# Banded attention in a two-layer trunk: mask matmuls ahead of the scores, next pair's scores ahead of this pair's values, two value banks

## The chip, the cores and the metric

One core of a Trainium2 chip runs the whole program. The metric is device time in microseconds (us), the median of several executions. The engines are TensorE (PE, with its weight loads as PEld), VectorE (DVE), ScalarE (ACT), GpSimd (POOL) and SyncE (SP), which issues the weight DMAs.

## What is computed

Two layers of a decoder trunk, 512 tokens by 1024 channels in f32. Each layer mixes tokens by three branches side by side, then runs an MLP:

```python
o_a = mla_branch(...) @ w_o_mla          # 8 heads, causal
o_b = swa_branch(q_swa, k_swa, v_swa, positions, swa_sinks) @ w_o_swa   # the banded branch
o_c = stick_breaking_branch(...) @ w_o_sb
x = x + rms_norm((g0 * o_a + g1 * o_b + g2 * o_c) @ w_out)
x = x + rms_norm(square(relu(rms_norm(x) @ w_up)) @ w_down)
```

The banded branch has 8 query heads of 64 channels, a window of 128 tokens, and one learned sink for each head:

```python
s = einsum(q, k) * HEAD_DIM ** -0.5          # a block of 128 queries sees itself and the block before
s = where(valid, s, -inf)
m = maximum(max(s), sink)
p = exp(s - m); p = p / (sum(p) + exp(sink - m))
o = einsum(p, v)
```

## The kernel before

Every engine's instruction list is written out by hand, and engines meet through counting semaphores. Nothing reorders the work: an engine that waits holds all that is queued behind it. Every f32 matmul is three matmuls of high and low parts (`three`), so most operands need a high part, written by ACT, and a low part, written by DVE. Weights stream through a ring of four chunks. `split` on ACT writes the high part of a chunk (128x1024), `split` on DVE the low part.

The **banded stage** lies between the eight causal heads and the stick-breaking stage. Its heads are called m = 0 to 7 here, in four pairs t = 0 to 3. The program's `n` in this stage is 2t. Beside the heads, PE runs two output tiles of the causal branch (`out_tile(0, ..)`) and one projection tile of 24 matmuls for each pair. The work on one head goes round the engines like this:

- PE, `band_scores(t)`: scores of both heads of a pair. Their matmuls use 64 rows of the array each, and the heads alternate between the two halves. Masks are added by matmuls of 128 rows with an identity.
- DVE, `band_biggest(m)`: four instructions for the maximum over the score banks (`bmx`). POOL then reduces it over partitions (`bmxr`), and PE subtracts it from the scores (`band_shift(m)`).
- ACT, `soft_exp` (`bs_f`) and `band_hi` (`bp_hi`). DVE, `band_lo` (`bp_lo`). There is one `bp_hi` and one `bp_lo`: `band_hi(m)` waits until `band_values(m-1)` on PE has read them.
- PE, `band_values(m)`: values into half a bank, and the sum of the probabilities into the other half.
- DVE, `band_den(m)`: adds `sink_exp(m)` of ACT to that sum. ACT, `soft_out(m)`: logarithm and exponential of it (`dn`). DVE, `soft_out(m)`: their product with the values (`of`), which frees the value bank. After each odd head `out_hi` on ACT and `out_lo` on DVE split `of`.
- `mixed` on DVE multiplies an output tile by its gate and frees the tile's bank.

POOL's maximum for head m also waits for `sink_exp(m-2)`. Eight PSUM banks exist. Banks 2 to 5 hold the scores of a pair, bank 6 (`pv_bank`) the values, and bank 7 the results of `rotate`, which turns query channels for the rotary part (`rope`, `rope_in`, `rope_turn`, `rope_out` on ACT and DVE). In the stick-breaking stage bank 7 holds scores again. That stage starts on DVE with `stick_min(0)` and `stick_min(1)`, and its first values matmul (`stick_values(0)`, L885) waits for the low part of its probabilities (`p_lo`), which is at the end of a chain over DVE and ACT.

## Time and profile before

| | |
|---|---|
| median of 3 runs | 1734.01 us (1733.11 to 1734.31) |
| the profiled execution's own time | 1734.41 us |
| its span, first to last instruction | 1732.6 us |
| PE busy | 98% of the span |
| DVE, ACT, POOL busy | 64%, 49%, 8% |
| mean granted TensorE clock | 0.997 of full speed |
| banded stage, first layer | about 162 to 240 us of the span |
| banded stage, second layer | about 1018 to 1096 us of the span |

Busy shares are averages over the whole span. Matmuls overlap each other's ends in the records, so the distance between the starts of two matmuls is what one costs in a stream. The same holds for DVE and ACT: the start-to-start distance is the cost in a queue, and the duration counts when another engine waits.

### The profile page before, as it was taken

What the parts mean: (1) busy time and instruction counts of PE and PEld (TensorE: products, weight loads), DVE (VectorE), ACT (ScalarE), POOL (GpSimd) and SP (SyncE); (2) the same over time, 40 slices, a digit from 0 to 9 for tenths busy, and PEclk for the clock granted to TensorE, in tenths of its full rate; (3) what the DMA queues carried; (4) which work ended last, traced back from release to release, by engine and by line L of the source; (5) the groups of instructions that cost most, each with busy time, mean ns of one, the idle gap of its engine ahead of it and who ended that gap; (6) DMA issues with size and microseconds to landing.
All of it is one profiled execution on the core that took longest, in us unless ns stands there. A gap on an engine that the chain in (4) does not pass through costs nothing.

```text
span 1732.6 us, 21793 instructions
## 1 busy us (share of the span) xinstructions
PE 1704.3 (98%) x8585; PEld 1437.6 (83%) x8585; DVE 1107.1 (64%) x1498; ACT 854.7 (49%) x1203; POOL 142.0 (8%) x140
## 2 busy tenths in 40 slices
PE   9999999999999999999999999999999999999997
PEld 6888888888898888888888888888888988888886
DVE  8887887775566534364587777877754665344545
ACT  7576666665355414131466755666644554232223
POOL 0111211111100000000001111111111000000000
PEclk9999999999999999999999999999999999999999
DMA  4121121222432222222321211122224122222222
GB/s 149 67 73 59 60 74 62 77 75 80 138 118 74 97 98 97 98 98 97 119 82 65 76 61 61 61 74 74 74 85 164 68 98 97 98 97 98 97 98 73
DMA packets 47495, 152.09 MB, mean 88 GB/s; under 512 B 5153, under 2 KB 9633, under 8 KB 47394
## 3 DMA queue, kind: packets, MB, share of 16 engines
q1 hardware_dynamic: 45664, 147.42, 24.5%
q10 hardware_dynamic: 1730, 3.28, 0.5%
q8 instruction: 68, 1.11, 0.3%
q14 instruction: 33, 0.27, 0.1%
HBM read 146.49 MB, written 4.19 MB: 87 GB/s over the span
## 4 chain that ended last, share of the span: by engine, by line
PE 83%; issue 7%; DVE 6%; ACT 3%; POOL 1%; DMA 1%; DVEq 0%; SPq 0%; ACTq 0%; POOLq 0%
PE bank L579 77%; PE bank L584 3%; PE bank L834 1%; PE bank L885 1%; POOL mix L2303 1%; ACT w_hi L1039 1%; DVE w_lo L1582 0%; DVE h_lo L1617 0%; DVE hf L1629 0%; PE bank L588 0%; DMA x<-in_x 0%; PE bank L687 0%; DVE x L1638 0%; DVE fb L1828 0%; ACT dn L1096 0%
## 5 line engine op out<-in xcount | busy, mean ns | idle before, releaser
L579 PE MATMUL bank<-h_hi,w_hi 128*128 128x512 f32 (+1 forms) x1224 | 477.7, 390 | 4.6 <-DVE h_lo L1617 2.4
L579 PE MATMUL bank<-h_hi,w_lo 128*128 128x512 f32 (+1 forms) x1224 | 472.3, 386 | 0.0
L579 PE MATMUL bank<-h_lo,w_hi 128*128 128x512 f32 (+1 forms) x1224 | 472.3, 386 | 0.0
L1039 ACT ACTIVATE w_hi<-raw 128x1024 fp32r<-128x1024 f32 (+2 forms) x269 | 271.0, 1013 | 220.0 <-DMA raw<-in_w 219.6
L1582 DVE TENSOR_TENSOR w_lo<-raw,w_hi 128x1024 fp32r<-128x1024 f32 (+2 forms) x269 | 316.8, 1181 | 63.3 <-ACT w_hi L1039 56.9
L579 PEld LDWEIGHTS bank<-h_hi,w_hi 128*128 128x128 f32 x1224 | 230.4, 188 | 54.8 <-issue 5.7
L579 PEld LDWEIGHTS bank<-h_hi,w_lo 128*128 128x128 f32 x1224 | 230.3, 188 | 46.9
L579 PEld LDWEIGHTS bank<-h_lo,w_hi 128*128 128x128 f32 x1224 | 230.5, 188 | 45.2 <-issue 1.7
L579 PE MATMUL bank<-u_hi,w_hi 128*128 128x512 f32 (+1 forms) x560 | 208.0, 371 | 0.0
L579 PE MATMUL bank<-u_hi,w_lo 128*128 128x512 f32 (+1 forms) x560 | 207.7, 371 | 0.0
L579 PE MATMUL bank<-u_lo,w_hi 128*128 128x512 f32 (+1 forms) x560 | 207.7, 371 | 0.0
L579 PEld LDWEIGHTS bank<-u_lo,w_hi 128*128 128x128 f32 x560 | 105.5, 188 | 18.3
L579 PEld LDWEIGHTS bank<-u_hi,w_hi 128*128 128x128 f32 x560 | 105.5, 188 | 18.1
L579 PEld LDWEIGHTS bank<-u_hi,w_lo 128*128 128x128 f32 x560 | 105.5, 188 | 18.0
L1903 DVE TENSOR_TENSOR usq<-relu 128x512 f32<-128x512 f32 x64 | 44.3, 692 | 104.0 <-ACT relu L1243 103.4
L1243 ACT ACTIVATE relu<-bank 128x512 f32<-128x512 f32 x48 | 28.6, 596 | 139.0 <-PE bank L579 139.0
L1921 DVE TENSOR_TENSOR y<-bank,y 128x512 f32<-128x512 f32 x32 | 22.1, 692 | 98.7 <-PE bank L579 98.7
L579 PE MATMUL bank<-o_hi,w_hi 128*128 128x512 f32 x192 | 76.5, 398 | 0.0
L1245 ACT ACTIVATE u_hi<-relu 128x512 fp32r<-128x512 f32 x64 | 40.5, 633 | 70.1 <-DVE relu L1898 68.6
L579 PE MATMUL bank<-o_hi,w_lo 128*128 128x512 f32 x192 | 74.9, 390 | 0.0
L579 PE MATMUL bank<-o_lo,w_hi 128*128 128x512 f32 x192 | 74.8, 390 | 0.0
L2303 POOL TENSOR_TENSOR mix<-mix,gate 128x512 f32<-128x512 f32 x32 | 44.4, 1391 | 357.0 <-DVE gate L1878 357.0
(264 smaller groups left out, 2747.3 us busy)
## 6 DMA issues: line engine op xcount, KB each, us to landing
raw<-in_w SPq DMA_DIRECT2D x251, 512.0 KB, 3.2
x<-in_x SPq DMA_DIRECT2D x16, 256.0 KB, 3.3
side_raw<-in_w SPq DMA_DIRECT2D x6, 512.0 KB, 4.8
x_spill<-x ACTq DMA_DIRECT2D x8, 256.0 KB, 2.5
x<-x_spill SPq DMA_DIRECT2D x8, 256.0 KB, 3.2
out_y<-x SPq DMA_DIRECT2D x8, 256.0 KB, 2.1
raw<-in_w SPq DMA_DIRECT2D x8, 192.0 KB, 2.4
raw<-in_w SPq DMA_DIRECT2D x8, 128.0 KB, 2.3
```

Source lines behind the costliest of these rows:

```text
L579: mm = pe.matmul(o, s, m, start=start and i == 0 and j == 0, stop=last and i == n - 1 and j == 2, skip_group_check=True)
L584: return pe.matmul(o, stationary, moving, start=False, stop=True, skip_group_check=True)
L834: return pe.matmul(to[:, off + col:off + col + w], a, m, start=(r, n, i) in STICK_STARTS, stop=i == 2, skip_group_check=True)
L885: mm = pe.matmul(pv_bank[:, q0:q0 + w], v[:, j, h % 2, :], part[:, s], start=i == 0 and part is p_hi, stop=part is p_lo, skip_group_check= ...
L1039: act.activation(chunk_in(gc, w_hi, side_hi)[:, 0:w], chunk_in(gc, raw, side_raw)[:, 0:w], ACT.Copy)\
L1243: act.activation(relu[:, n % 2, :], tile_bank(name)[:, :], ACT.Relu).then_inc(free_of(name), 1)
L1245: act.activation(u_hi[g % 2][:, t, :], relu[:, n % 2, :], ACT.Square).then_inc(u_h.sem, 1)
L1582: dve.tensor_tensor(chunk_in(gc, w_lo, side_lo)[:, 0:w], chunk_in(gc, raw, side_raw)[:, 0:w], chunk_in(gc, w_hi, side_hi)[:, 0:w].bitcast( ...
L1903: dve.tensor_tensor(usq[:, n % 2, :], relu[:, n % 2, :], relu[:, n % 2, :], ALU.mult)\
L1921: ins = dve.tensor_tensor(y[:, t, :], tile_bank(name)[:, :], y[:, t, :], ALU.add)
L2303: pool.tensor_tensor(mix[:, t, :], mix[:, t, :], gated_at(b, t), ALU.add).then_inc(mix_add.sem, 1)
```

## The change

The diff touches four things. The masks of a pair are written first, with `start=True`, and the score matmuls add to them. `band_scores(t+1)` stands ahead of `band_values(n)` and `band_values(n-1)` behind `out_tile(0, n)`. Heads 0, 2 and 4 put their values in bank 7, the others in bank 6. ACT and DVE get another order, in which the normalisation of a head stands later and the splits of the weights behind both exponentials. `rotate(2)` moves into the middle of a projection tile.

```diff
+        def values_bank(n):
+            return bank[7] if n - HEADS in (0, 2, 4) else pv_bank
+        def values_bank_free(n):
+            m = n - HEADS
+            if m in (0, 2):
+                return rot_used(m // 2 + 4)
+            return pv_free(n - 1 if 0 < m < 6 else n)
...
                 def band_scores(t):
+                    pe.wait_ge(*p_exp(banks_of(HEADS + 2 * t)))
+                    for r in range(2):
+                        add(band[r][0][:, :].rearrange("p (a c) -> p a c", a=2), cst[:, IDENT, :],
+                            both.unsqueeze(1).broadcast_to([P, 2, 2 * P]), start=True)
+                        add(band[r][1][:, 0:2 * P], cst[:, IDENT, :], both, start=True)
+                        add(band[r][1][:, 2 * P:3 * P], cst[:, IDENT, :], cst[:, MASK_CAUSAL, :])
                     pe.wait_ge(*rpo_l(t + 2))
-                    pe.wait_ge(*p_exp(banks_of(HEADS + 2 * t)))
...
 # stick_scores(0)
+                        pe.wait_ge(*pv_free(HEADS + 5))
...
 # PE, the stage
-                    rotate(2)
-                    tile(("swa_q", 2), h_hi, h_lo)
+                    tile(("swa_q", 2), h_hi, h_lo, None, lambda: rotate(2))
                     for t in range(PAIRS):
                         n = 2 * t
+                        out_tile(0, n)
                         if t:
                             band_values(n - 1)
-                        out_tile(0, n)
                         band_shift(n)
                         out_tile(0, n + 1)
                         band_shift(n + 1)
...
+                            band_scores(t + 1)
                         band_values(n)
-                        if t + 1 < PAIRS:
-                            band_scores(t + 1)
...
 # ACT, the stage
-                            soft_out(HEADS + n - 1)
+                            band_hi(n - 1)
+                            soft_out(HEADS + n - 2)
+                            sink_exp(n - 1)
                         soft_exp(HEADS + n)
                         band_hi(n)
+                        if t:
+                            soft_out(HEADS + n - 1)
+                        sink_exp(n)
+                        soft_exp(HEADS + n + 1)
                         if t:
                             out_hi(HEADS + n - 1)
                         split(C["o", 0, t] + 2)
...
-                        soft_exp(HEADS + n + 1)
-                        sink_exp(n)
...
+                    band_hi(HEADS - 1)
+                    soft_out(2 * HEADS - 2)
+                    sink_exp(HEADS - 1)
...
 # DVE, the stage: see its rows below; behind its loop
+                    band_lo(HEADS - 1)
+                    band_den(HEADS - 2)
+                    soft_out(2 * HEADS - 2)
```

PE's list around the scores of pair 1, before: the scores with their masks in two places (`cst` is the identity), then the values of head 1.

```order
L806 MATMUL bank<-wq_hi,wk_hi 128x256 [waits p_exp,rope_out_lo]
...
L806 MATMUL bank<-wq_hi,wk_lo 128x256 x2
L584 MATMUL bank<-cst 128x512 x2
L806 MATMUL bank<-wq_hi,wk_hi 128x256 x2
...
L806 MATMUL bank<-wq_hi,wk_lo 128x128 x2
L584 MATMUL bank<-cst 128x256
L584 MATMUL bank<-cst 128x128
L584 MATMUL bank<-cst 128x256
L584 MATMUL bank<-cst 128x128
L579 MATMUL bank<-bp_hi,wv_hi 128x256 [waits pv_free,p_lo_ready]
```

The same place in the changed kernel.

```order
L595 MATMUL bank<-cst 128x512 [waits p_exp]
L595 MATMUL bank<-cst 128x256
L595 MATMUL bank<-cst 128x128
L595 MATMUL bank<-cst 128x512
L595 MATMUL bank<-cst 128x256
L595 MATMUL bank<-cst 128x128
L825 MATMUL bank<-wq_hi,wk_hi 128x256 [waits rope_out_lo]
...
L825 MATMUL bank<-wq_hi,wk_lo 128x256 x2
...
L825 MATMUL bank<-wq_hi,wk_lo 128x128 x2
L590 MATMUL bank<-bp_hi,wv_hi 128x256 [waits rot_used,p_lo_ready]
```

The six mask matmuls stand in front of the first wait for the rotated queries. The scores then run without a break, and the values that follow are those of head 0, which wait for bank 7 instead of bank 6.

DVE's list for pair 1 before, from the maximum of head 2 to the end of the two splits (`dn<-bank,dn` is `band_den`, `of` is `soft_out`, `mix` is `mixed`, `w_lo` the splits).

```order
L1692 TENSOR_TENSOR bmx_125<-bank,bmx_125 128x128 [waits max_step,score_full]
L1782 TENSOR_TENSOR dn<-bank,dn 64x512 [waits sink_exp,pv_full]
L1688 TENSOR_SCALAR bmx_126<-bank,vec_all 128x256 [waits score_full,max_all]
...
L1692 TENSOR_TENSOR bmx_126<-bank,bmx_126 128x128 [waits max_step,score_full]
L1791 TENSOR_TENSOR mix<-bank,mix 128x512 [waits mix_gate,tile_full]
L1701 TENSOR_TENSOR of<-bank,dn 64x512 [waits o_lo_ready,den_inv]
L1669 TENSOR_TENSOR bp_lo<-bs_f_121,bp_hi 128x896 [waits p_hi_ready]
L1708 TENSOR_TENSOR o_lo_82<-of,o_hi_81 128x512 [waits o_hi_ready]
L1582 TENSOR_TENSOR w_lo<-raw,w_hi 128x1024 [waits w_hi_ready] x2
L1791 TENSOR_TENSOR mix<-bank,mix 128x512 [waits mix_gate,tile_full]
L1767 TENSOR_TENSOR rb<-bank,cf 128x512 [waits rope_sum,rotated]
```

The same pair in the changed kernel.

```order
L1706 TENSOR_TENSOR bmx_125<-bank,bmx_125 128x128 [waits max_step,score_full]
L1683 TENSOR_TENSOR bp_lo<-bs_f_122,bp_hi 128x896 [waits p_hi_ready]
L1796 TENSOR_TENSOR dn<-bank,dn 64x512 [waits sink_exp,pv_full]
...
L1706 TENSOR_TENSOR bmx_126<-bank,bmx_126 128x128 [waits max_step,score_full]
L1715 TENSOR_TENSOR of<-bank,dn 64x512 [waits o_lo_ready,den_inv]
L1805 TENSOR_TENSOR mix<-bank,mix 128x512 [waits mix_gate,tile_full]
L1796 TENSOR_TENSOR dn<-bank,dn 64x512 [waits sink_exp,pv_full]
L1683 TENSOR_TENSOR bp_lo<-bs_f_121,bp_hi 128x896 [waits p_hi_ready]
L1715 TENSOR_TENSOR of<-bank,dn 64x512 [waits o_lo_ready,den_inv]
L1722 TENSOR_TENSOR o_lo_82<-of,o_hi_81 128x512 [waits o_hi_ready]
L1805 TENSOR_TENSOR mix<-bank,mix 128x512 [waits mix_gate,tile_full]
L1596 TENSOR_TENSOR w_lo<-raw,w_hi 128x1024 [waits w_hi_ready] x2
```

The low part of head 1 (`bp_lo<-bs_f_122`) now lies between the two maxima. `out_lo` (`o_lo_82`) and `mixed` of the second tile stand in front of the splits, and both products `of` stand behind the second maximum.

ACT's list for the same pair before (`bs_f` is `soft_exp`, the two rows on `dn<-dn` are `soft_out`, `dn<-bmxr` is `sink_exp`, `o_hi` is `out_hi`, `w_hi` the splits).

```order
L1094 ACTIVATE dn<-dn 64x512 [waits pv_free,denominator]
L1096 ACTIVATE dn<-dn 64x512 [waits den_inv]
L1123 ACTIVATE bs_f_121<-bank 128x512 [waits score_shifted,p_lo_ready]
...
L1130 ACTIVATE bp_hi<-bs_f_121 128x896 [waits pv_full,p_exp]
L1112 ACTIVATE o_hi_81<-of 128x512 [waits pv_free]
L1039 ACTIVATE w_hi<-raw 128x1024 [waits loaded2]
L1039 ACTIVATE w_hi<-raw 128x1024 [waits loaded3]
L1123 ACTIVATE bs_f_122<-bank 128x512 [waits score_shifted,p_lo_ready]
...
L1105 ACTIVATE dn<-bmxr_127,vec_all 64x512 [waits den_inv,max_all]
```

The same pair in the changed kernel.

```order
L1140 ACTIVATE bp_hi<-bs_f_122 128x896 [waits pv_full,p_exp]
L1104 ACTIVATE dn<-dn 64x512 [waits pv_free,denominator]
...
L1115 ACTIVATE dn<-bmxr_128,vec_all 64x512 [waits den_inv,max_all]
L1133 ACTIVATE bs_f_121<-bank 128x512 [waits score_shifted,p_lo_ready]
...
L1140 ACTIVATE bp_hi<-bs_f_121 128x896 [waits pv_full,p_exp]
L1104 ACTIVATE dn<-dn 64x512 [waits pv_free,denominator]
L1106 ACTIVATE dn<-dn 64x512 [waits den_inv]
L1115 ACTIVATE dn<-bmxr_127,vec_all 64x512 [waits den_inv,max_all]
L1133 ACTIVATE bs_f_122<-bank 128x512 [waits score_shifted,p_lo_ready]
...
L1122 ACTIVATE o_hi_81<-of 128x512 [waits pv_free]
L1049 ACTIVATE w_hi<-raw 128x1024 [waits loaded2]
L1049 ACTIVATE w_hi<-raw 128x1024 [waits loaded3]
```

`soft_out`, `sink_exp` and the second `soft_exp` now stand in front of `out_hi`, and the splits behind all of them.

## Rows read from the trace of the kernel before

**Rows 1.** Waits of PE, whole span: total us, times, longest.

```profile
PE bank L885 <- issue: 2.7, 2, 1.3
...
PE bank L579 <- DVE of L1701: 1.9, 6, 0.5
...
PE bank L834 <- ACT bs_f L1123: 1.2, 2, 0.6
```

**Rows 2.** Timeline of PE, pair 1: start us, duration, instruction, idle before.

```profile
184.12 0.28 PE L579 MATMUL bank<-bp_hi,wv_hi 128*128 128x256 f32 x1
...
185.37 0.27 PE L579 MATMUL bank<-bp_hi,wv_lo 128*128 128x128 f32 x1
185.58 0.38 PE L806 MATMUL bank<-wq_hi,wk_hi 64*128 64x256 f32 x2
185.80 0.28 PE L806 MATMUL bank<-wq_lo,wk_hi 64*128 64x256 f32 x2
...
186.48 0.73 PE L584 MATMUL bank<-cst 128*128 128x512 f32 x2
187.14 0.39 PE L806 MATMUL bank<-wq_hi,wk_hi 64*128 64x256 f32 x2
...
187.97 0.68 PE L584 MATMUL bank<-cst 128*128 128x256 f32 x4
189.16 0.36 PE L579 MATMUL bank<-bp_hi,wv_hi 128*128 128x256 f32 x1 [0.51 <-DVE of L1701]
```

**Rows 3.** Timelines of POOL and PE at the shift of head 1.

```profile
175.79 1.78 POOL L2292 PARTITION_ALL_REDUCE bmxr<-bmx  x1 [5.88 <-DVE bmx L1692]
...
177.63 0.69 PE L584 MATMUL bank<-bmxr,cst 128*128 128x256 f32 x4
```

**Rows 4.** Timeline of DVE, one of each kind of instruction.

```profile
188.94 1.06 DVE L1688 TENSOR_SCALAR bmx<-bank,vec_all 128x256 fp32r<-128x256 f32 x2
...
190.95 0.69 DVE L1782 TENSOR_TENSOR dn<-bank,dn 64x512 f32<-64x512 f32 x1
...
197.50 2.35 DVE L1582 TENSOR_TENSOR w_lo<-raw,w_hi 128x1024 fp32r<-128x1024 f32 x2
...
200.37 0.68 DVE L1767 TENSOR_TENSOR rb<-bank,cf 128x512 f32<-128x512 f32 x1
...
203.26 0.69 DVE L1663 SCALAR_TENSOR_TENSOR tmp<-bank,rstd_x 128x512 f32<-128x512 f32 x1
...
236.91 0.68 DVE L1791 TENSOR_TENSOR mix<-bank,mix 128x512 f32<-128x512 f32 x1
237.63 0.70 DVE L1782 TENSOR_TENSOR dn<-bank,dn 64x512 f32<-64x512 f32 x1
238.36 1.09 DVE L1669 TENSOR_TENSOR bp_lo<-bs_f,bp_hi 128x896 fp32r<-128x896 f32 x1
```

**Rows 5.** Timeline of ACT, one of each kind of instruction.

```profile
193.89 0.98 ACT L1123 ACTIVATE bs_f<-bank 128x512 f32<-128x512 f32 x2 [0.91 <-PE bank L584]
194.90 0.95 ACT L1130 ACTIVATE bp_hi<-bs_f 128x896 fp32r<-128x896 f32 x1
195.76 0.61 ACT L1112 ACTIVATE o_hi<-of 128x512 fp32r<-128x512 f32 x1
...
205.66 0.63 ACT L1094 ACTIVATE dn<-dn 64x512 f32<-64x512 f32 x1
...
206.98 0.72 ACT L1105 ACTIVATE dn<-bmxr,vec_all 64x512 f32<-64x512 f32 x1
```

**Rows 6.** Timelines of DVE, then PE, from the first `stick_min` to `stick_values(0)`.

```profile
240.30 3.13 DVE L1819 TENSOR_SCALAR fb<-bank 128x512 f32<-128x512 f32 x6
...
251.24 0.69 DVE L1663 SCALAR_TENSOR_TENSOR tmp<-bank,rstd_x 128x512 f32<-128x512 f32 x1 [0.50 <-PE bank L579]
...
266.92 1.49 DVE L1669 TENSOR_TENSOR p_lo<-fb,p_hi 128x1280 fp32r<-128x1280 f32 x1 [0.33 <-ACT p_hi L1201]
...
268.51 0.47 PE L885 MATMUL bank<-p_hi,sb_v 128*128 128x512 f32 x1 [1.34 <-issue]
```

More of the change, by code:

```diff
@@ L742, in values @@
                             probs = p_hi[:, s], p_lo[:, s]
-                        mm = three(pv_bank[:, q0:q0 + w], [(vals(j), probs)], start=i == 0)
+                        mm = three(values_bank(n)[:, q0:q0 + w], [(vals(j), probs)], start=i == 0)
                     mm.then_inc(pv_full.sem, 1)
@@ L1700, in soft_out @@
                     own = rows if n < HEADS else slice(0, HEAD)
-                    dve.tensor_tensor(of[rows, :], pv_bank[own, :], dn[own, :], ALU.mult)\
+                    dve.tensor_tensor(of[rows, :], values_bank(n)[own, :], dn[own, :], ALU.mult)\
                        .then_inc(pv_free.sem, 1)
@@ L2112, in _ @@
                         if t:
-                            band_den(n - 1)
+                            band_lo(n - 1)
+                            band_den(n - 2)
+                        band_biggest(n + 1)
+                        if t:
+                            soft_out(HEADS + n - 2)
                         else:
@@ L2133, in _ @@
                             stick_scaled(0, t - 1)
-                        band_den(n)
-                        band_lo(n + 1)
-                        soft_out(HEADS + n)
-                        if 0 < t < 3:
                             stick_in_low(0, t - 1)
+                    band_lo(HEADS - 1)
+                    band_den(HEADS - 2)
+                    soft_out(2 * HEADS - 2)
                     for p in range(PAIRS):
```

34 lines of the change are left out of this document (13 added, 21 removed).

## The prediction

> **What bounds the kernel now.** PE is busy for 98% of the span, so a change in this stage is worth what it takes from PE's stream, or from whatever PE waits for at the end of it. I read the waits of PE over the whole span first. The reader is to see how little there is, and where [rows 1]: 1.9 us before `band_values`, put down to the product that frees the one value bank, 1.2 us at the start of the stick-breaking scores, and 2.7 us at `stick_values(0)`. Each occurs in both layers, and the timelines of both layers agree within some tenths of a us, so I work on the first layer and double the result.
>
> Second, PE's own timeline through pair 1 [rows 2]. It shows small gaps that count as busy. From the last values matmul (185.37) to the first score matmul (185.58) it is 0.21 us, and to the next weights (185.80) 0.22, where a 256-column matmul costs 0.12 and a 128-column one 0.11. So passing between 128-row and 64-row matmuls costs about 0.1 for the switch and 0.1 for the restart, 0.2 in all. It happens four times for each pair: scores, masks (186.48), scores (187.14), masks (187.97).
>
> Third, the end. `stick_values(0)` starts at 268.51 after 1.34 us without a matmul [rows 6]. The `p_lo` it needs starts at 266.92 and takes 1.49. DVE's chain to that point starts with `stick_min(0)` at 240.30, and its last wait for PE is at 251.24 (0.50 us, for a projection tile). From there on DVE and ACT only wait for each other. So what PE gains in the banded stage reaches the end only if DVE's `stick_min(0)` also comes earlier, and if it comes more than 0.5 us later, the rest is lost on the path. This wait decides the change, and it ends last at DVE.
>
> **PE's part of the change.** Masks first leaves two of four switches: 4 pairs x 2 x 0.2 = 1.6 us in a layer. The waits before `band_values` go (about 1 us in a layer), and the wait before the stick-breaking scores may (0.6) [rows 1]. The masks also cover a short wait before pair 0's scores, and `rotate(2)` inside a tile covers another, together about 0.8 by the gaps of PE there, the least certain term. PE's side is thus worth up to 4 us in a layer. No matmul is added or removed.
>
> The Trainium skill, TensorEngine Tiling (Array Packing), under Key Properties, says that a change of tiling mode drains TensorE. The rows agree, with the 0.2 us above, and it would favour this change; it says nothing of who waits next.
>
> **Where pair 0 returns its gain.** The shift of head 1 waits for POOL: its reduction runs 175.79 to 177.57 and the shift starts at 177.63 [rows 3]. DVE reaches that maximum by instructions which the change leaves in order, none of which waits for PE. So PE arrives earlier and waits, and the tile ends where it ended, 184.12 [rows 2]. All of pair 0's lead is gone.
>
> **Walk through pair 1.** Costs: maximum 2.01 (188.94 to 190.95), two splits 2.27, one rotary turn with the copy to ACT and `mixed` 2.89 (200.37 to 203.26), `mixed` 0.6 if the next may overlap it [rows 4]. ACT: two exponentials 1.01, `band_hi` 0.95, `soft_out` 1.32, sink 0.75, `out_hi` 0.52 before the next and 0.61 to its end [rows 5]. Handing over between engines costs 0.04 to 0.1.
>
> From 184.12: masks 0.86 (the 1024 and 768 columns of [rows 2] without the restarts), switch 0.1, scores 1.44: they end at 186.51 (before: 188.5). Values of head 0 run to 188.18. Head 1: `band_hi` 188.28 to 189.23, `band_lo` 189.27. DVE has finished the maximum of head 2 by then, so this start is set by PE and ACT. From here the new order binds:
>
> - `band_lo(1)` then `band_den(0)`. Does the second overlap the first? [rows 4] show `mixed` (0.68) then `band_den` at +0.72 and `band_den` (0.70) then `band_lo` at +0.73: no overlap around an instruction on the upper 64 rows. So 1.09 + 0.04 = 1.13, and `band_den(0)` ends at 190.40 + 0.69 = 191.09. With overlap (0.6 kept as for other pairs, a saving of 0.08 to 0.12) it would be 190.97. I take the first.
> - ACT then does, without a gap, `soft_out(0)`, sink, exponential, `band_hi`, `soft_out(1)`, sink, exponential: 1.32 + 0.75 + 1.01 + 0.98 + 1.32 + 0.75 + 0.98 = 7.11, plus 0.04. `out_hi(1)` starts at 198.24, and DVE, which has nothing to do from about 197.2, gets `out_lo(1)` at 198.89. That is a wait of 1.6 us that DVE did not have.
> - `out_lo` 0.6, `mixed` 0.6, splits from 200.1 to 202.37, rotary turn without `mixed` 2.89 to 205.26, `tmp` and the copy on ACT 1.40, low part 0.6: the maximum of head 4 starts at 207.27.
>
> In the kernel before, that maximum starts only after the same instructions and PE's scores, about a us later. But PE now has the scores of pair 2 at 204.2, and DVE is 3 us behind it. Pair 2's `band_lo(3)` comes at 207.27 + 2.01 = 209.28 and ends at 210.4, while PE, with values and an output tile, stands at `band_values(3)` from 208.5: a new wait of about 1.9.
>
> The Trainium skill, VectorE: DVE Perf Modes, in the section on two Vector instructions with no wait between them, says that an instruction starts only after all earlier ones when its start quadrant differs from theirs. The rows around `band_den` agree with it. By the rule the three `band_lo`, `band_den` pairs give 5.0 us in all for the two layers; with overlap they give 4.4.
>
> **The added waits.** `rotate(4)` now waits for the product of head 0 (193.6, PE comes at 195.8), and behind it stand a tile and scores. Head 2's values wait for the first step of the rotary turn (203.1, PE comes at 204.3). `stick_scores(0)` waits for the product of head 4 (230.4, PE at about 235). All three are hidden by 1.2 us or more. SP's list is not touched; a weight chunk is fetched when PE has done with the one four before, so its fetch moves with PE. The splits stand up to 2.5 us later on DVE, and are done 2 to 3 us before PE asks for them.
>
> **Pairs 2 and 3.** The same chain from maximum to maximum: 2.01 + 1.13 + 0.69 (end of `band_den`) + 7.15 + 0.65 (`out_lo`) + 1.2 + 2.27 + 1.4 + 0.6 = 17.1. Maximum of head 6 at 224.4. PE, with its waits behind it, stands ready again for pair 3. Pair 3 has no `tmp`: its splits end at 224.4 + 15.1 = 239.5. Now `band_lo(7)`, `band_den(6)` and `soft_out(6)` stand behind the splits, where before they stood among PE's last tiles: 1.13 + 0.69 + 0.04 + 1.31 (ACT) + 0.04 + 0.61 = 3.8. `stick_min(0)` starts at 243.3, against 240.30: 3.0 late. PE also waits before `band_values(6)`, since heads 5, 6 and 7 share bank 6 and `soft_out(5)` ends near 234.5; it still starts the stick-breaking scores some 0.5 earlier than before, and that lead is worth nothing.
>
> **Sum.** 3.0 late at `stick_min(0)`, less 0.5 that DVE waited for PE at 251.24 [rows 6], is 2.5 at `p_lo` and at `stick_values(0)`. Behind it PE's stream has no gap of that size in this layer, so it stays. Two layers: +5.0 on the profiled execution's 1734.4, 1739.4; the median before is 0.4 lower, so 1739.0. The bounds of each handover (0.04 or 0.1, overlap or not, ten of them in a layer) move it by 0.8 a layer: +3.4 to +6.6. Errors in my durations lean to neither side, and I give 1738.8.
>
> **Rivals.**
> - **PE's gains stand (faster).** If DVE and ACT keep up, that is if the chain above takes 15 us and not 17.1 from maximum to maximum, `stick_min(0)` comes with PE. PE gains up to 4 in a layer, of which pair 0's 1 or so is lost at POOL: -3 in a layer, 1728; with a part of it 1731. For it: DVE is busy 64% over the span only, and 1.6 us of my chain is one wait. Against: DVE's own instructions for pair 1 sum to 16.6 us (maxima 4.0, low parts 2.2, `band_den` 1.4, products 1.3, `mixed` 1.3, `out_lo` 0.6, splits 2.3, turn 2.2, inputs of the next stage 1.3) of a period near 18. It decides where `out_lo` waits less than 0.3 us. Chance 0.15.
> - **A wash.** DVE is late by 0.5 to 2.2 at `stick_min(0)`, which the waits at 251.24 and a shorter chain nearly take up: 1734 to 1737.4. It needs each pair 0.4 shorter than I have it. Chance 0.24.
> - **Worse.** The late DVE also delays `stick_tail` on PE and the weight splits behind it, so that a chunk is missing later: +8 or more, 1742. Chance 0.06.
> - My forecast, +3.5 to +7: 0.55.
>
> **Range and chances.** Bounds of the forecast 1737.4 to 1740.6; to leave out 2 in 10 I go to 1730 for most of the faster case and 1741.5. A measurement of this kernel tells 0.2%, 3.5 us, from no change. Slower by more than that 0.61, within it 0.25, faster 0.14.
>
> **What would show it.** Right: DVE waits over 1 us before `o_lo` in pairs 1 to 3 (it has no such wait before); PE waits at `band_values(3)` and `band_values(6)`; `stick_min(0)` near 243 and `stick_values(0)` near 271; six masks in a row before each pair's scores. Wrong: `stick_min(0)` before 241, or no wait before `o_lo`. What would make it wrong most easily is ACT: if its seven instructions overlap more than [rows 5] show, each pair gives back up to 1 us.

## The result, and the profile after

The changed kernel takes 1742.5 us (median of 4 executions, 1742.3 to 1743.4); the kernel before took 1733.6 in the same turns. The ratio is 1.0052, with a 95% interval of 1.0037 to 1.0066: 8.9 us slower. The forecast was 1738.8 with a range of 1730 to 1741.5, so the sign was right and the size was outside the range.

All times of a trace count from its own start, and the trace of after shows the first rows of the banded stage 0.62 us earlier than that of before, for reasons ahead of the stage. I add 0.62 where I compare the two.

The head of the page after:

```profile
span 1740.5 us, 21785 instructions
PE 1700.2 (98%) x8585; PEld 1437.1 (83%) x8585; DVE 1107.6 (64%) x1498; ACT 855.0 (49%) x1203; POOL 143.6 (8%) x140
```

The shares of busy time are those of before. What moved is which waits there are. The waits of PE over the whole span, as in [rows 1] (total, times, longest):

```profile
PE bank L590 <- DVE ra L1774: 4.8, 2, 2.6
...
PE bank L590 <- DVE bp_lo L1683: 3.3, 4, 1.5
PE bank L590 <- DVE of L1715: 3.1, 2, 1.6
PE bank L897 <- issue: 2.7, 2, 1.3
PE bank L595 <- DVE sp_lo L1860: 2.6, 2, 1.3
PE bank L590 <- DVE tmp L1675: 2.6, 2, 1.3
```

Before, all of these but the `issue` row were absent or under 2 us. Every new row names DVE. Two were forecast (`bp_lo` at `band_values(3)`, `of` at `band_values(6)`). `sp_lo` and `tmp` belong to the stick-breaking stage, which is late. The largest, `ra` (a step of `rope_in`, which frees a tile's bank), was not forecast. PE's timeline shows the place of each in the first layer (start, duration, instruction, idle before):

```profile
175.22 0.47 PE L590 MATMUL bank<-o_hi,w_hi 128*128 128x512 f32 x1 [2.23 <-DVE ra L1774]
...
184.45 1.02 PE L595 MATMUL bank<-cst 128*128 128x512 f32 x6
185.40 0.39 PE L825 MATMUL bank<-wq_hi,wk_hi 64*128 64x256 f32 x2
...
210.67 0.39 PE L590 MATMUL bank<-bp_hi,wv_hi 128*128 128x256 f32 x1 [1.47 <-DVE bp_lo L1683]
228.74 0.39 PE L590 MATMUL bank<-bp_hi,wv_hi 128*128 128x256 f32 x1 [0.17 <-DVE bp_lo L1683]
235.66 0.36 PE L590 MATMUL bank<-bp_hi,wv_hi 128*128 128x256 f32 x1 [1.47 <-DVE of L1715]
259.58 0.50 PE L595 MATMUL bank<-sp_hi,cst 128*128 128x512 f32 x1 [1.31 <-DVE sp_lo L1860]
263.11 0.47 PE L590 MATMUL bank<-h_hi,w_hi 128*128 128x512 f32 x1 [1.29 <-DVE tmp L1675]
272.22 0.47 PE L897 MATMUL bank<-p_hi,sb_v 128*128 128x512 f32 x1 [1.33 <-issue]
```

The six masks stand in a row at 184.45, as the change has it. The last row is `stick_values(0)`, as in the last of [rows 6]: 272.22 + 0.62 = 272.84, against 268.51. The first layer is 4.3 us longer at this point; twice that is 8.6 of the 8.9.

DVE's timeline. The first two rows, of pair 0's rotations, stand behind the maximum of head 1, which starts at 167.33; the others are rows that I had walked through:

```profile
169.24 0.68 DVE L1781 TENSOR_TENSOR rb<-bank,cf 128x512 f32<-128x512 f32 x1
...
174.39 0.68 DVE L1774 SCALAR_TENSOR_TENSOR ra<-bank,cf 128x512 f32<-128x512 f32 x1
...
199.44 0.69 DVE L1722 TENSOR_TENSOR o_lo<-of,o_hi 128x512 fp32r<-128x512 f32 x1 [1.72 <-ACT o_hi L1122]
...
224.62 1.07 DVE L1702 TENSOR_SCALAR bmx<-bank,vec_all 128x256 fp32r<-128x256 f32 x2
...
226.84 1.85 DVE L1683 TENSOR_TENSOR bp_lo<-bs_f,bp_hi 128x896 fp32r<-128x896 f32 x1 [0.23 <-ACT bp_hi L1140]
...
243.87 0.68 DVE L1715 TENSOR_TENSOR of<-bank,dn 64x512 f32<-64x512 f32 x1 [1.36 <-ACT dn L1106]
...
270.63 1.49 DVE L1683 TENSOR_TENSOR p_lo<-fb,p_hi 128x1280 fp32r<-128x1280 f32 x1 [0.34 <-ACT p_hi L1211]
```

The wait of 1.72 before `o_lo` occurs in all of pairs 1 to 3 (forecast 1.6). `band_den` starts 1.12 us behind the `band_lo` of head 3 (210.65 behind 209.53), so the two do not overlap, as I had taken it. `stick_min(0)`, the next instruction after 243.87, starts at 244.48; with 0.62 that is 245.1, where I had 243.3. From there to `p_lo` it is 26.15 us, against 26.62 before: the late start saved the 0.5 that I had counted on.

### The profile page after: what moved, and what is told of

It is laid out like the page before. It is cut to its first block, busy times and chain, and to the rows that moved or that the text cites. A ratio compares the mean times of both kernels' runs of the same rounds, so it can differ in the third digit from the quotient of the medians.

```text
span 1740.5 us, 21785 instructions
## 1 busy us (share of the span) xinstructions
PE 1700.2 (98%) x8585; PEld 1437.1 (83%) x8585; DVE 1107.6 (64%) x1498; ACT 855.0 (49%) x1203; POOL 143.6 (8%) x140
## 3 DMA queue, kind: packets, MB, share of 16 engines
q10 hardware_dynamic: 1730, 3.28, 0.5%
## 4 chain that ended last, share of the span: by engine, by line
PE 77%; DVE 8%; issue 8%; ACT 5%; POOL 1%; DMA 1%; DVEq 0%; ACTq 0%; SPq 0%; POOLq 0%
PE bank L590 72%; PE bank L595 2%; DVE w_lo L1596 1%; PE bank L897 1%; PE bank L846 1%; POOL mix L2320 1%; ACT w_hi L1049 1%; DVE fb L1842 0%; DVE h_lo L1631 0%; DVE hf L1643 0%; PE bank L599 0%; ACT dn L1106 0%; ACT dn L1104 0%; ACT bs_f L1133 0%; DVE bmx L1702 0%
```

## The experiments

There are two theories. **A:** PE does its part of the change, but VectorE's and ScalarE's new order is late, and that is what costs. **B:** PE's new order and the shared bank cost by themselves. Theories named C are about single rows: GpSimd's all-reduce and the VectorE instructions beside it.

Each run is numbered in the order in which it ran, and was timed in turns with the kernel before on its own chip; I give the median, and the ratio with its 95% interval where the verdict rests on it. Runs on different chips are compared by these; where the difference is small, I also give the place of a row in both traces. In the diffs a line with - is what the kernel named first has.

### 1. The rotation ahead of the second maximum in pair 0

This is the only place where my walk and the rows part in pair 0: the change has `band_biggest(1)` ahead of `rope_turn(2)` and the two steps behind it, not behind them.

```diff
                         band_biggest(n)
+                        if t == 0: rope_turn(2, ...); split(C["swa_q", 2] + 2); rope_in(3, ...)
                         band_biggest(n + 1)
-                        else: rope_turn(2, ...); split(C["swa_q", 2] + 2); rope_in(3, ...)
```

> The changed kernel with one thing put back: in pair 0, VectorE does the rotary turn of the second query pair, its weight split and the next rotary input ahead of the maximum of head 1, as before the change. Theory A (VectorE's and ScalarE's new order is the cost; in pair 0 it frees the bank that the second output tile needs 2 us later): the wait of 2.2 us before the second output tile goes, the shift of head 1 comes about 1.0 us earlier in each layer, and since all behind it hangs on that, the time falls by 2 us, to about 1740.5. Theory B (TensorE's new order and the sharing of value banks are the cost): that wait is made up elsewhere, within 0.5 us of the changed kernel, 1742.5.

Measured: 1740.8 us, 1.8 less than the change. PE's timeline in pair 0, where the change had the wait of 2.23:

```profile
173.66 0.47 PE L590 MATMUL bank<-o_hi,w_hi 128*128 128x512 f32 x1 [0.33 <-DVE ra L1774]
...
177.35 0.68 PE L595 MATMUL bank<-bmxr,cst 128*128 128x256 f32 x4 [0.72 <-POOL bmxr L2309]
```

The second output tile starts at 173.66 instead of 175.22 (1.9 us sooner, this trace's rows of the stage standing 0.35 later than those of after), and the shift of head 1 waits for POOL, as in my walk. The waits of 1.72 at `o_lo`, of 1.36 at `of` and the slow `bp_lo` stay. `stick_values(0)` comes 0.9 us earlier in the first layer. So the order in pair 0 is 1.8 us of the 8.9.

### 2. to 4. PE's side by itself

Run 2 puts the masks first in the kernel before and changes nothing else. Run 3 is the changed kernel's PE order and banks with ScalarE and VectorE in the order of before. Run 4 is the changed kernel with the masks back in two places.

```diff
 # run 2, band_scores of the kernel before; run 4 is the same edit backwards in the changed kernel
+    for r in range(2):
+        add(band[r][0]..., both..., start=True); add(band[r][1]...)
     scores, start=False
-    masks behind block 0, masks behind block 1
```

> The kernel before with the masks written first and nothing else changed. Theory A: TensorE saves two switches of 0.2 us for each of 8 pairs, VectorE's chain in the kernel before follows TensorE in each pair, so most of it is kept: 1 to 3 us faster, about 1731.5. Theory B, in which TensorE's stream decides everything: 3.2 us faster, 1730.4. No gain at all would say that the switches are not what they look like in the rows.

> TensorE's list of the changed kernel (masks first, scores ahead of values, two value banks), with the order of ScalarE and VectorE of the kernel before. Theory A in its simple form, that the other engines' order alone costs: faster than the kernel before, by up to 6 us. By a walk through the chain it should not be: the maximum of the next pair then stands behind the normalisation of the first head, whose values now come behind the scores, so VectorE starts it some 5 us after the scores and TensorE waits about 3 us at the shift of each pair; 1745 to 1755. Theory B: slower by about what the changed kernel is, 1742.

> The changed kernel with the masks put back behind the scores, in two places. Theory A: TensorE's stream loses 0.4 us for each of 8 pairs, 3.2 us, but TensorE is the one that waits in this stage, so only pair 1, where the chain starts from the values of head 0, passes it on: 0.5 to 1.5 us slower than the changed kernel, about 1743.5. Theory B: all 3.2 us, 1745.7.

Measured: run 2 took 1733.7 us (ratio 1.0000, 0.9991 to 1.0009) and run 4 1742.6, as the change. The 0.4 us per pair that the masks' order saves turned into longer waits. PE's waits in run 2, to be read against 1.9 before for `of` and 0.6 for `rp_lo`:

```profile
PE bank L579 <- DVE of L1699: 5.1, 6, 1.0
...
PE bank L794 <- DVE rp_lo L1753: 2.5, 2, 1.3
```

Run 3 took 1757.3 us (ratio 1.0138, 1.0124 to 1.0151), 23.8 above before. Neither theory had said that; the walk in the same expectation had, with 1745 to 1755, and was 2 us short. Its waits of PE, then VectorE's row in pair 1:

```profile
PE bank L595 <- POOL bmxr L2302: 20.4, 8, 3.4
```

```profile
209.98 0.69 DVE L1792 TENSOR_TENSOR dn<-bank,dn 64x512 f32<-64x512 f32 x1 [3.27 <-PE bank L590]
```

In the old order VectorE does `band_den`, `band_lo` and `soft_out` of a pair ahead of the next pair's first maximum. PE's new order brings the values for that `band_den` behind the next scores. So the first maximum starts only at 213.55, some 5 us behind the end of the scores, and POOL's all-reduce and the shift of the even head are late with it. The windows of run 3 (the stretch and its length, busy time of PE, PEld, DVE, ACT, POOL, then the granted clock, DMA share, GB/s) show a second cost:

```profile
211.00:216.00 5.00, 3.11 (x20) 2.67 (x18) 4.41 (x8) 1.99 (x3) 0.37 (x1) 1.00 0.00 0
216.00:221.00 5.00, 3.54 (x12) 2.92 (x13) 4.16 (x8) 4.16 (x7) 3.19 (x2) 0.73 0.00 0
```

Behind a wait of 3.35 us (it ends at 217.46) the granted clock is 0.73 over the second of the two stretches. How the 23.8 us divide between waits and clock was not measured. So the new order of VectorE and ScalarE is not an extra on PE's new order: without it PE's order is far worse. Theory A in its simple form (undo their part and the kernel is fast) is wrong; PE waits for them with that order, and much longer without it.

### 5. Masks and both banks in the old order

```diff
 # the kernel of run 2
-    pv_bank for every head
+    values_bank(n), values_bank_free(n), and the waits in rotate(4) and stick_scores(0), as in the change
```

> The kernel before with two parts of the change alone: masks ahead of the scores, and the values of a pair's two heads in two banks. Every engine keeps the order of before. In the run with masks first alone, TensorE's waits at the value bank grew from 1.9 to 5.1 us over both layers (for VectorE's product `of`), which swallowed what the masks saved. Theory A (those waits are for the bank, and the second bank takes them away; VectorE's and ScalarE's new order alone made the change slow): the 5.1 us fall to about 1, and the kernel is 2 to 4 us faster than before, 1730 to 1732. Theory B (TensorE waits there for VectorE's and ScalarE's chain itself, whichever bank it writes; the wait moves to bp_lo or the next scores): within 1 us of before, 1733 to 1734.5, with as many us of waits under other names.

Measured: 1732.9 us (ratio 0.9996, 0.9987 to 1.0004). The waits for `of` are gone, and one for POOL has come in their place (0.2 in the trace of before, and in run 2's). PE's waits are now:

```profile
PE bank L595 <- POOL bmxr L2304: 3.5, 7, 0.7
...
PE bank L807 <- DVE rp_lo L1767: 2.5, 2, 1.3
```

So the bank by itself was not what held PE. The waits name what PE gets back from VectorE, directly or by way of POOL, and that is so in the kernel before already. VectorE is not simply full there: in pair 2 of this trace it waits 2.37 us itself, for PE's projection tile. The rows point to the round from PE's tile over ScalarE and VectorE back to PE, in which the masks have no part. Which link of it sets the pace before the change was not tested.

### 6. Head 7 ahead of both splits in the last pair

```diff
 # run 1; ScalarE and VectorE, last pair
-    out_hi / out_lo(5), split, split, band(7), denominator of head 6
+    out_hi / out_lo(5), band(7), denominator of head 6, split, split
```

> The run with the rotation first (1740.8) with one edit more: in the last pair, band_hi of head 7 and the logarithm of head 6's denominator on ScalarE, and band_lo(7) and band_den(6) on VectorE, stand ahead of the two weight splits instead of behind them. Theory A (VectorE's wait of 1.36 us at `of` of head 6, and ScalarE's splits ahead of band_hi(7), lie on the path to stick_min(0), and that to the end of the layer): stick_min(0) 1.4 us earlier per layer, TensorE's wait of 1.46 at values(6) shorter, 1737 to 1739. Rival (the splits that now come later hold up the stick tile, or the path goes by the stick scores on TensorE): no change within 0.5 us, 1740.8, or slower.

Measured: 1742.5 us, 1.7 slower than run 1. The rival held, and the order that I had written is the cause: ScalarE reached the splits only at 240.55, behind the two steps of the denominator, and VectorE waited for them.

```profile
238.62 0.70 DVE L1800 TENSOR_TENSOR dn<-bank,dn 64x512 f32<-64x512 f32 x1
241.62 2.36 DVE L1600 TENSOR_TENSOR w_lo<-raw,w_hi 128x1024 fp32r<-128x1024 f32 x2 [2.31 <-ACT w_hi L1049]
```

A wait of 1.36 became one of 2.31.

### 7. The first split where ScalarE idles

```diff
 # run 1; pairs 1 to 3
 ScalarE:
     band_hi(n - 1)
+    split(C["o", 0, t] + 2)
     soft_out ... out_hi(n - 1)
-    split(C["o", 0, t] + 2)
 VectorE:
     soft_out(n - 1)
-    out_lo(n - 1); mixed(n + 1); split(C["o", 0, t] + 2)
+    mixed(n + 1); split(C["o", 0, t] + 2); out_lo(n - 1)
```

> The run with the rotation first (1740.8) with one edit more: in pairs 1 to 3 ScalarE does the first of the two weight splits right behind band_hi(n-1), where it idles 2 to 3.5 us, and VectorE does its half of it and the mixing product ahead of out_lo instead of behind it, in the 1.7 us in which it waits for o_hi. Theory A (VectorE is what is late in pairs 1 to 3): the three waits of 1.72 at o_lo go, each following maximum is up to 1.7 us earlier, TensorE's waits of 1.49 at values(3) and 1.46 at values(6) go; 2.5 to 4 us per layer, 1733 to 1736, about the kernel before. Rival (those waits on VectorE cost nothing since it waits for TensorE's scores next): 1739.5 to 1740.8.

Measured: 1733.8 us (ratio 1.0000, 0.9991 to 1.0009), 7.0 less than run 1. VectorE's row in pair 1, to be read against the 199.44 of after:

```profile
197.98 0.69 DVE L1724 TENSOR_TENSOR o_lo<-of,o_hi 128x512 fp32r<-128x512 f32 x1
```

All three waits before `o_lo` are gone, and PE's at `band_values(3)`; the one at `band_values(6)` is 1.32. This is the largest step of all, it touches neither PE nor a bank, and it takes away the wait that I had forecast as 1.6. That shows theory A's mechanism: in pairs 1 to 3 the change is late by the time that VectorE spends waiting for `o_hi`.

### 8. A second all-reduce behind each one

```diff
 # the changed kernel, band_maximum on GpSimd
     pool.partition_all_reduce(bmxr..., bmx..., max)
+    pool.wait_ge(*mx_all(n + 1))
+    pool.partition_all_reduce(scratch[:, 0:256], constants, max)
```

> The changed kernel, with a second all-reduce on GpSimd behind each of the eight of the banded stage, over 256 columns of constants into a scratch tile that nothing reads. Theory C (an operation of VectorE whose operands all lie in SBUF runs slower while GpSimd does an all-reduce; one that reads a PSUM bank does not): the bp_lo, w_lo, and wq_lo that lie under the added all-reduces take 1.3 to 1.9 times as long as elsewhere, the maxima (1.07 and 0.82) do not change, and the kernel is 1 to 4 us slower than the change. Rival (the 1.85 us of bp_lo in the change had another cause, as its two-way split over a tile that ScalarE writes): the same durations as in the change, and its time within 0.5 us.

Measured: 1742.2 us, as the change. Theory C in this form failed: `bp_lo` at 217.33, which lies under an added all-reduce but for its first 0.05 us, took 1.09. But that all-reduce took 1.97 and not the 1.06 of others of its kind in this trace. VectorE's row, then POOL's:

```profile
217.33 1.09 DVE L1684 TENSOR_TENSOR bp_lo<-bs_f,bp_hi 128x896 fp32r<-128x896 f32 x1
```

```profile
215.51 1.78 POOL L2310 PARTITION_ALL_REDUCE bmxr<-bmx  x1 [0.19 <-ACT dn L1116]
217.38 1.97 POOL L2314 PARTITION_ALL_REDUCE scratch<-cst  x1
```

This says that the later of the two is held. The rival, another cause for the 1.85, stands until runs 13 and 17.

### 9. to 12. From run 7 to the fastest

Each run adds one edit to the one before it. Run 9: VectorE's half of the second split in the last pair goes into its wait of 1.36. Run 10: pair 0's third rotation goes ahead of a split. Run 11: pair 0's splits go ahead of the exponential of head 1, as they stood before the change.

```diff
 # 9, VectorE, last pair
-    split(stick_vt + 2); band_lo(7); band_den(6)
+    band_lo(7); band_den(6); split(stick_vt + 2)
 # 10, pair 0, VectorE (ScalarE alike, rope(3) ahead of the split)
-    split(swa_q2 + 2); rope_in(3); band_biggest(1)
+    rope_in(3); band_biggest(1); split(swa_q2 + 2)
 # 11, pair 0
 ScalarE:  band_hi(0); + both splits; sink_exp(0); soft_exp(1); - both splits
 VectorE:  band_lo(0); + first split; mixed(1); - first split
```

> The run with the splits early (1733.8) with one edit more, on VectorE alone: in the last pair its half of the second weight split (1.15 us) moves from ahead of bp_lo of head 7 to behind band_den(6), where VectorE waits 1.36 us for ScalarE's reciprocal of head 6. ScalarE's order stays, so that w_hi is there. Theory A (VectorE's row up to stick_min(0) sets the end of the stage, also after the splits moved): stick_min(0) 1.1 us earlier per layer, 1731 to 1732.2. Rival (TensorE is the bound again, since it waits only 5 us per layer in the stage, and the time found there is lost in front of the stick stage): 1733.2 to 1733.8.

> The run before this one (last split later) with one edit more, in pair 0: the third rotation's first step stands ahead of the weight split of swa_q2 + 2 on ScalarE and VectorE, and that split behind band_biggest(1) on VectorE. So the tile bank of swa_q2 comes free and the maximum of head 1 ends 1.1 us earlier. Theory A: TensorE's waits of 0.34 for `ra` and 0.73 for GpSimd's maximum of head 1 go, all behind them 0.8 to 1.1 us earlier per layer, 1.5 to 2 us less than the run before this one. Rival (the wait moves to mixed(0), w_lo or scores(1)): within 0.5 us of it.

> The run before this one with one edit more, in pair 0: ScalarE does both weight splits ahead of the exponential of head 1, as the kernel before did, and VectorE its half of the first one ahead of mixed(1). VectorE's wait of 1.95 us for w_hi goes. Theory A, with VectorE late in pair 0: up to 1 us per layer less. Rival (in pair 0 VectorE waits for TensorE's scores of pair 1 in any case): within 0.5 us of the run before this one; TensorE shows no wait in pair 0 in either.

Measured: 1732.9, 1732.0 and 1731.6 us; the last has the ratio 0.9989 (0.9980 to 0.9997). Run 9 gave 0.9, between its theory and its rival: the wait of 1.36 went, and one of 1.05 for `bp_hi` of head 7 came in front of it, since ScalarE still does its half of the split (the first row) ahead of `band_hi(7)`:

```profile
233.93 1.04 ACT L1049 ACTIVATE w_hi<-raw 128x1024 fp32r<-128x1024 f32 x1
234.88 0.94 ACT L1140 ACTIVATE bp_hi<-bs_f 128x896 fp32r<-128x896 f32 x1
```

Run 10 took away the wait for `ra` and brought the maximum of head 1 forward, but left PE's 0.73 for POOL, and gave 0.9 of the 1.5 to 2 (run 17 shows why). Run 11 gave 0.4, as its rival had it. In the traces `stick_values(0)` comes 0.30, 0.49 and 0.15 us earlier for each of the three in the first layer (counted from `wq_lo` at the start of the stage, which is at 161.46 before and at 160.84 after).

Run 12 is run 11 with the masks back in two places (the edit of run 4).

> The fastest run so far (pair 0 splits early, 1731.6) with one part of the change undone: the masks again behind the scores, in two places of each pair. The same edit on the changed kernel itself moved nothing (1742.6 against 1742.5). Theory A (the masks' order saves TensorE two switches of about 0.2 us per pair, and that counts only once VectorE and ScalarE are not what is late): 8 pairs by 0.4, so 2 to 3.2 us slower than with the masks first, 1733.5 to 1735. Rival (the masks' order is worth nothing in any surroundings): within 0.5 us, 1731 to 1732.

Measured: 1734.9 us, ratio 1.0004 (0.9995 to 1.0013) to a kernel before that took 1734.2 on this chip, against 0.9989 for run 11. The difference of the ratios is 0.15%, or 2.6 us; of the medians 3.3. The two intervals just overlap, but the traces say the same: `stick_values(0)` stands 107.78 us behind that `wq_lo` in run 12 and 106.04 in run 11, 1.7 more in one layer. The edit that moved nothing in run 2 and in run 4 is worth 2.6 to 3.3 here, about the 8 pairs by 0.4 us of my second step. One row of each shows the order, run 11 first:

```profile
182.82 1.02 PE L595 MATMUL bank<-cst 128*128 128x512 f32 x6
```

```profile
185.40 0.73 PE L595 MATMUL bank<-cst 128*128 128x512 f32 x2
...
186.90 0.68 PE L595 MATMUL bank<-cst 128*128 128x256 f32 x4
```

### 13. to 16. The slow low part in the last pair

In the change `bp_lo` at 226.84 starts 0.13 us behind an all-reduce and takes 1.85. Theory C2 is that the first 0.90 us of an all-reduce and a VectorE instruction with two SBUF inputs exclude each other. Run 13 moves `bp_lo` to another distance by an exchange with the instruction behind it. Run 14 does that in run 11, in pairs 1 and 3.

```diff
 # 13: the changed kernel, last pair; 14: run 11, pairs 1 and 3
     band_biggest(n)
-    band_lo(n - 1); band_den(n - 2)
+    band_den(n - 2); band_lo(n - 1)
     band_biggest(n + 1)
```

> The changed kernel with two instructions of VectorE in the last pair exchanged: band_den(4) ahead of band_lo(5). In the change bp_lo starts 0.13 us behind the start of GpSimd's all-reduce of head 6 and takes 1.85 us. Theory C2 (the all-reduce keeps bp_lo, whose two inputs both lie in SBUF, from reading for its first 0.90 us; dn, which reads a bank, is not held): bp_lo now starts 0.6 to 0.75 behind the all-reduce, takes 1.25 to 1.4 and ends at the same time, and band_biggest(7) and all behind it come 0.7 us earlier: 1.4 us less than the change, 1741 to 1741.5. Rival (bp_lo is slow for another reason, or is held for the whole of the all-reduce): bp_lo takes 1.85 again or ends with the all-reduce, TensorE waits 0.5 us longer at values(5), and the time is 1742.5 or more.

> The fastest run so far (pair 0 splits early) with the same exchange in pairs 1 and 3, where VectorE waits 1.16 and 0.95 us for bp_hi ahead of bp_lo: band_den(n-2) stands in that wait. Theory A (VectorE's row still counts at the end of the stage): stick_min(0) 0.7 us earlier per layer, 0.5 to 1.4 us less, 1730.2 to 1731. Rival (after the splits moved, TensorE's own row and its wait of 1.33 us for the product `of` at values(6) set the end): that wait shrinks by 0.7 too if theory A holds, and stays 1.33 if not; time within 0.5 of 1731.6.

The profiled execution of run 13 took 1740.3 us and shows POOL's row, then VectorE's:

```profile
226.14 1.78 POOL L2312 PARTITION_ALL_REDUCE bmxr<-bmx  x1 [11.33 <-DVE bmx L1706]
```

```profile
226.08 0.69 DVE L1796 TENSOR_TENSOR dn<-bank,dn 64x512 f32<-64x512 f32 x1
226.80 1.32 DVE L1683 TENSOR_TENSOR bp_lo<-bs_f,bp_hi 128x896 fp32r<-128x896 f32 x1
```

`bp_lo` now starts 0.66 behind the all-reduce and takes 1.32; `dn`, which reads a PSUM bank, took its usual 0.69. But the median of run 13 was 1743.7, since four of its five executions had a mean granted clock of 0.995 or 0.996. So it ran again, in turns with the changed kernel itself (run 16, no edit).

> The same kernel as the run with band_den first in pair 3. Its profiled execution took 1740.3 us at a mean granted clock of 0.997, its four others 1743.2 to 1744.7 at 0.995 to 0.996. Theory C2 with the clock as a separate matter (the exchange saves 0.7 us per layer; the clock fell in some executions): executions at 0.997 or 0.998 lie at 1740 to 1741.5, those at 0.995 near 1744. Rival (the exchange saves nothing, the profiled execution was a stray one): all executions 1742.3 or more, whatever their clock.

> The changed kernel itself, on the same chip and in turns with the run before it. Its first four executions took 1742.3 to 1743.4 at 0.997 to 0.998. If the lower clock comes from the chip and not from the order, it shows here too, as 1744 to 1747 at 0.995; if it comes from the exchange, this stays at 1742.3 to 1743.4.

Measured: run 15 1741.2 us, with four executions of 1740.5 to 1742.3 at 0.997 and one of 1744.5 at 0.995. Run 16, the change, 1743.9, with two of 1742.4 and 1742.5 at 0.998 and three of 1743.9 to 1744.4 at 0.996. Sorted by mean clock, the exchange saves 1 to 2 us: 1740.3 to 1742.3 at 0.997 against 1742.3 to 1743.4 at 0.997 and 0.998. Without sorting, the ten executions of runs 13 and 15 and the nine of the change have the same median, 1742.7. So the times by themselves do not show the saving; the traces of runs 13 and 15, both at full clock in this stage, do: `stick_min(0)` comes 0.7 us earlier than in the change. The lower clock belongs to the change as well. Its place is in the trace of run 16, behind the 2.24 us in which PE waits for `ra`. PE's timeline, and the windows:

```profile
175.19 0.54 PE L590 MATMUL bank<-o_hi,w_hi 128*128 128x512 f32 x1 [2.24 <-DVE ra L1774]
175.52 0.63 PE L590 MATMUL bank<-o_lo,w_hi 128*128 128x512 f32 x1
175.95 0.63 PE L590 MATMUL bank<-o_hi,w_lo 128*128 128x512 f32 x1
...
178.91 0.39 PE L590 MATMUL bank<-o_hi,w_hi 128*128 128x512 f32 x1
179.13 0.39 PE L590 MATMUL bank<-o_lo,w_hi 128*128 128x512 f32 x1
```

```profile
175.00:180.00 5.00, 4.81 (x16) 3.90 (x17) 1.84 (x4) 0.66 (x1) 0.00 (x0) 0.66 0.02 3
```

From 175.5 to 178.5 a matmul of 512 columns comes every 0.43 us, where it is 0.23 from 178.91 on: the clock is at the lower of its two levels, 1.2 instead of 2.4 GHz, for eight of them, which costs 8 x 0.2 = 1.6 us. It began behind the wait. The trace of run 8 shows it too, behind 1.89 us (0.66 in that window). In the traces of the change, of run 13 and of run 15 the wait of 2.23 is there and the clock 1.00 in that window, and in the second layer, where PE waits 2.6 us for `ra`, no trace of these kernels shows it. So the lower clock came behind that wait in some executions and not in others.

Run 14 took 1729.8 us, ratio 0.9975 (0.9965 to 0.9985), 1.8 less than run 11; PE's wait at `band_values(6)` is 0.85 instead of 1.33, and `stick_values(0)` comes 0.9 us earlier in the first layer.

### 17. The same exclusion from the other side

In runs 10, 11, 12 and 14 VectorE's split starts 0.17 to 0.18 us ahead of the all-reduce of head 1, and that takes 2.68 or 2.69. Run 17 exchanges two instructions of run 14.

```diff
 # VectorE, pair 0
     band_biggest(1)
-    split(swa_q2 + 2); mixed(0)
+    mixed(0); split(swa_q2 + 2)
```

> The fastest run so far (best with the denominator first, 1729.8) with one exchange in pair 0 on VectorE: mixed(0), which reads a bank, ahead of the weight split of swa_q2 + 2, which reads two tiles in SBUF. In that run the split starts 0.18 us ahead of GpSimd's all-reduce of head 1, which then takes 2.68 us and not 1.78, and TensorE waits 0.73 us for it. Theory C2 (an instruction with two SBUF inputs and the reading part of an all-reduce exclude each other, and the later one is held): the all-reduce takes 1.78, the split, now 0.4 us behind its start, takes 1.6 to 1.75, TensorE's wait of 0.73 goes, and all behind comes up to 0.7 us earlier per layer, 1728.4 to 1729.3. Rival (the 2.68 had another cause, or VectorE's row sets the rest): the all-reduce still takes 2.5 or more, or the time stays at 1729.6 to 1730.

Measured: **1727.9 us, ratio 0.9967 (0.9955 to 0.9979)**, the fastest: 5.6 us less than the kernel before. POOL's row of run 10, then POOL's and VectorE's of run 17:

```profile
174.37 2.68 POOL L2315 PARTITION_ALL_REDUCE bmxr<-bmx  x1 [4.51 <-DVE bmx L1708]
```

```profile
174.46 1.78 POOL L2321 PARTITION_ALL_REDUCE bmxr<-bmx  x1 [4.51 <-DVE bmx L1709]
```

```profile
174.28 0.68 DVE L1808 TENSOR_TENSOR mix<-bank,mix 128x512 f32<-128x512 f32 x1
174.88 1.70 DVE L1599 TENSOR_TENSOR w_lo<-raw,w_hi 128x1024 fp32r<-128x1024 f32 x1
```

The all-reduce is back at 1.78, the split is held instead (1.70 for 1.22), and PE's timeline shows no wait in pairs 0 to 2. `stick_values(0)` comes 0.93 us earlier than in run 14, in one layer; the median says 1.9 for both, while the two ratios' intervals overlap.

## Why the prediction was wrong in size

These are its own steps, for the first layer.

- **Where pair 0 returns its gain: the step that failed.** "DVE reaches that maximum by instructions which the change leaves in order." The change puts the maximum of head 1 ahead of the rotation, the split and the next rotation's input. The reading of the order was wrong, not a duration. The shift does not wait for POOL; the output tile ahead of it waits 2.23 us for `ra`, which frees its bank. All behind it is 1.0 us later per layer than I had it. Run 1 gave 1.8 us for both layers, and the shift of head 1 then came where it came before. In some executions the lower clock behind that wait adds 1.6 us (run 16).
- **Walk through pair 1: right** (forecast in brackets). The wait at `o_lo` is 1.72 (1.6), and it is 18.95 us from head 1's `band_hi` to the maximum of head 4 (18.99). PE's wait at `band_values(3)` is 1.47 (1.9): the low part ended 0.8 us later than I had it, and PE came there 1.3 later. The error in pair 0 does not explain that difference, since run 1, without it, shows 1.49.
- **Pair 2: right.** It is 17.0 us from maximum to maximum (17.1).
- **Pair 3: mis-sized.** From the maximum of head 6 to `stick_min(0)` it is 19.86 us, where I had 18.9. Of the 0.96, 0.76 is `bp_lo` at 1.85 instead of 1.09, held by POOL's all-reduce, and 0.2 its wait for `bp_hi`. I had priced it at its time alone. The traces of runs 13 and 15 have 0.7 of it back.
- **The added waits: right.** None of the three shows in PE's waits. The exception that keeps heads 5, 6 and 7 in one bank shows, as forecast: 1.47 at `band_values(6)`.
- **Sum.** The 2.5 forecast, plus 1.0 and 0.8 to 0.96, is 4.3 to 4.5 per layer, against 4.3 seen. That the change is slower was not luck: the chain that was to make it so is there, and run 7, which breaks it, gives 7.0 us back.
- **PE's part: the masks right in size, and worth nothing here.** Run 12 measured them at 2.6 to 3.3 us for both layers where nothing hides them (3.2 forecast). The other terms of PE's side were not measured one by one. "What bounds the kernel now" held PE's stream to be the bound because it is busy 98% of the span. Run 2 contradicts that for this stage: with about 3.2 us less in PE's stream the kernel before took the same time.
- **The rivals.** "PE's gains stand" named its own condition rightly: it comes true where `out_lo` waits under 0.3 us. Run 7 makes it so, and the time falls by 7.0, to that of the kernel before; with all edits up to run 17 it is 1727.9, near the 1728 of that rival, but in an order that is not the change's.

What stays open: what decides whether the clock falls behind the 2.2 us wait. The first four executions of the change had a mean clock of 0.997 or 0.998, three of the next five 0.996, and only two of the nine were traced. Nor does any run give head 6 a value bank of its own in the new order; its wait for `of` (0.85 us in run 17) is the last one of PE in the banded stage.

The range was too narrow. It took in the errors of handing over, and neither a misread order (2.0 us over both layers) nor an instruction that another engine holds (1.5).

## What to carry to other kernels

Where an order is written out for each engine, the change of one engine's order is worth only what the engines that it waits for then allow. Look for a wait of such an engine on a further one (here 1.72 us at `o_lo`, three times a layer), and fill it with work that waits for nothing, such as the weight splits. Fill it on both engines: run 7, in which ScalarE did its half early, gained 7.0 us, and run 6, in which it did it late, lost 1.7. Do not start a VectorE instruction with two SBUF inputs right ahead of an all-reduce that TensorE waits for; put one that reads a bank there (run 17, 1.9 us). And test a gain of TensorE again after the others are in order: the same edit on the masks was worth 0.0 twice and then about 3 us.

When you predict such a change, write down the new order of every instruction of the engine that waits, from the difference of the orders, pair 0 included, before any duration. A stage whose waits of TensorE grow by what you take from its work, as in run 2, is not bound by TensorE, however busy it is.

## What the runs showed of the hardware

**A low part and an all-reduce exclude each other in part.** `bp_lo` reads two tiles in SBUF and takes 1.09 us by itself. Behind the start of GpSimd's all-reduce (1.78 us) it is held until about 0.90 us after that start: at a distance of 0.13 us it takes 1.85 (after), at 0.66 it takes 1.32 (run 13), at 0.85 it takes 1.13 (run 7). Distance and excess add up to 0.89 each time: 0.13 + 0.76, 0.66 + 0.23, 0.85 + 0.04; and 0.42 + 0.48 = 0.90 for the split of run 17. The other way round the all-reduce is longer: 1.97 against 1.06 when it starts 0.05 us behind `bp_lo` (run 8), and, in run 7:

```profile
206.82 2.55 POOL L2312 PARTITION_ALL_REDUCE bmxr<-bmx  x1 [12.67 <-DVE bmx L1708]
210.72 1.78 POOL L2312 PARTITION_ALL_REDUCE bmxr<-bmx  x1 [1.34 <-ACT dn L1115]
```

where `bp_lo` had started at 206.65. An instruction of VectorE that reads a PSUM bank kept its time beside an all-reduce (`dn`, 0.69, run 13). The Trainium skill, SBUF — State Buffer, under Who interferes with whom, says that a Vector instruction with two SBUF inputs contends with a GpSimd instruction that reads SBUF, and that issue order decides which of the two blocks. The rows agree on both. The page also says, of a Vector instruction in a 2-port mode, that whoever issues first keeps the shared ports for its whole instruction. The rows here, which are of another kind, show the all-reduce in the way for the first 0.90 us of its 1.78 alone.

**A wait of 2.2 us was followed by 1.6 us more in some executions.** Behind it the granted clock was at its lower level for eight matmuls in one trace of the change (0.66 over the 5 us) and not in another. In run 3 it was 0.73 in the window of 5 us behind the wait of 3.35 us (0.991 over the kernel, against 0.998 in the change).
